# Second block's first norm without its plain total, weight splits one pair at a time, sines inside the feed-forward

## The reference, cut to what matters

```
# first block
h = x + mix(rms_norm(x, mix_norm_w)) @ w_out
h = h + (silu(gate) * up) @ w_down        # gate, up = rms_norm(h, ffn_norm_w) @ w_gate_up, width 2816
x1 = rms_norm(h, final_norm_w)            # = h * fin * r1,  r1 = (mean(h^2) + EPS)^-0.5
# second block
shift1, scale1, gate1, shift2, scale2, gate2 = split(silu(c) @ ada_w + ada_b)
hn = rms_norm(x1, norm1_gain) * (1 + scale1) + shift1
r_q, r_k, r_v, r_g, s_q, s_k, s_v = split(hn @ w_in)
y = [retention(rotary(r_q), rotary(r_k), r_v) ..., stick_breaking(rms(s_q), rms(s_k), s_v)]
x  = x1 + gate1 * (y @ w_out)
x  = x + gate2 * peer(rms_norm(x, norm2_gain) * (1 + scale2) + shift2)   # 8 heads, top 16 of 16384 experts
```

## Time and profile before

| | us |
|---|---|
| median of 3 runs | 1205.56 |
| lowest, highest | 1204.44, 1211.71 |
| the profiled execution, its own time | 1207.72 |
| its span, first to last instruction | 1205.1 |
| PE busy | 1034.2 (86%) |
| DVE busy | 886.5 (74%) |
| ACT busy | 435.6 (36%) |
| POOL busy | 288.7 (24%) |
| DMA, mean over the span | 314 GB/s |

### The profile page before, as it was taken

The page is one execution under the profiler, slowest core; times in us unless marked ns, Lnnn a source line. Parts: engine busy times, 40 slices in busy tenths (PEclk is TensorE's granted clock), DMA queues, the critical chain, the costliest instruction groups (busy, mean ns, idle before and its releaser), DMA issues.

```text
span 1205.1 us, 14407 instructions
## 1 busy us (share of the span) xinstructions
PE 1034.2 (86%) x5140; PEld 720.2 (60%) x5140; DVE 886.5 (74%) x1809; ACT 435.6 (36%) x845; POOL 288.7 (24%) x260
## 2 busy tenths in 40 slices
PE   6998989999999998977989976887687768777987
PEld 6888889999988876964546432333233323333343
DVE  6976679998759785688478777667776776677545
ACT  6645454434446646443233222222211222122112
POOL 0000000000000000033435643544355335434530
PEclk9998999999999999988989988988898889888998
DMA  9532449979818331069999999999999999999994
GB/s 364 183 140 88 140 182 351 352 284 339 312 45 319 124 108 68 1 230 384 420 385 403 422 421 421 422 421 421 421 422 421 421 421 421 422 421 422 422 421 179
DMA packets 67751, 378.59 MB, mean 314 GB/s; under 512 B 7521, under 2 KB 7777, under 8 KB 34913
## 3 DMA queue, kind: packets, MB, share of 16 engines
q0 software_dynamic: 36864, 268.45, 53.8%
q1 hardware_dynamic: 29952, 107.13, 24.6%
q10 hardware_dynamic: 864, 2.10, 0.5%
HBM read 376.61 MB, written 1.05 MB: 313 GB/s over the span
## 4 chain that ended last, share of the span: by engine, by line
PE 32%; DVE 30%; DMA 25%; ACT 7%; issue 5%; POOL 1%; SPq 0%; ACTq 0%; DVEq 0%
DMA ring_sb<-in_peer,idsb 16%; DVE ring_lo L1316 5%; PE pb L851 5%; PE pb L412 5%; PE pb L415 5%; PE pb L854 5%; DMA whi_rows<-in_peer,idsb 4%; DVE ring_sb L1845 3%; PE pb L440 3%; DMA arena<-in_peer,idsb 3%; DVE arena L1584 2%; ACT whi L890 2%; DMA xn<-in_peer,idsb 2%; DVE arena L1788 1%; DVE arena L1783 1%
## 5 line engine op out<-in xcount | busy, mean ns | idle before, releaser
L1908 POOL DMA_INDIRECT ring_sb<-in_peer,idsb x143 | 164.5, 1151 | 735.3 <-DVE idsb L1828 528.7
L412 PE MATMUL pb<-xhi,whi 128*128 128x256 f32 x928 | 240.9, 294 | 5.3 <-ACT xhi L916 1.5
L851 PE MATMUL pb<-ring_sb,arena 128*128 128x512 f32 x286 | 164.2, 658 | 84.8 <-ACT arena L1257 84.7
L415 PE MATMUL pb<-xlo,whi 128*128 128x256 f32 x928 | 234.9, 287 | 0.9 <-DVE xlo L1758 0.3
L1845 DVE CUSTOM_DVE_ANT_0 ring_sb<-ring_sb,arena 128x1024 f32<-128x1024 f32 x143 | 172.2, 1224 | 84.7 <-DMA ring_sb<-in_peer,idsb 84.6
L412 PEld LDWEIGHTS pb<-xhi,whi 128*128 128x128 f32 x928 | 179.5, 193 | 11.7 <-issue 8.2
L415 PEld LDWEIGHTS pb<-xlo,whi 128*128 128x128 f32 x928 | 179.8, 194 | 6.1 <-issue 3.3
L1316 DVE TENSOR_TENSOR ring_lo<-ring_sb,whi 128x1024 fp32r<-128x1024 f32 x138 | 161.5, 1220 | 21.5 <-ACT whi L890 21.5
L1252 ACT ACTIVATE arena<-arena 128x4 f32<-128x4 f32 (+1 forms) x70 | 14.4, 205 | 416.0 <-DVE arena L1845 416.0
L854 PE MATMUL pb<-ring_sb,arena 128*128 128x512 f32 x286 | 158.5, 638 | 0.0
L851 PEld LDWEIGHTS pb<-ring_sb,arena 128*128 128x128 f32 x286 | 58.3, 212 | 162.4 <-issue 162.4
(11 more groups left out here) (320 smaller groups left out, 1619.1 us busy)
## 6 DMA issues: line engine op xcount, KB each, us to landing
ring_sb<-in_ada SPq DMA_DIRECT2D x48, 512.0 KB, 5.3
ring_sb<-in_w_gu SPq DMA_DIRECT2D x44, 512.0 KB, 6.8
ring_sb<-in_w_in SPq DMA_DIRECT2D x40, 512.0 KB, 7.1
ring_sb<-in_w_down SPq DMA_DIRECT2D x22, 512.0 KB, 5.8
ring_sb<-in_w_out SPq DMA_DIRECT2D x16, 512.0 KB, 3.5
ring_sb<-in_w_q SPq DMA_DIRECT2D x16, 512.0 KB, 6.3
ring_sb<-in_peer,idsb POOLq DMA_INDIRECT x143, 22.5
ring_sb<-in_w_iv SPq DMA_DIRECT2D x4, 512.0 KB, 16.6
```

What stands on the lines that cost most here:

```text
L412: e.matmul(o, hi_w(u)[:, c], xh(k), start=start, stop=False, skip_group_check=skip)
L415: e.matmul(o, hi_w(u)[:, c], xl(k), start=False, stop=False, skip_group_check=skip)
L851: mm = e.matmul(pb[4 + 2 * tile][:, :], dgr[col % 16], o[:, 1024:1536], start=begin, stop=end)
L1908: e.indirect_dma_start(rows_at[s], None, peer, bass.IndirectOffsetOnAxis(ap=idsb[:, col:col + 1], axis=0)).then_inc(s_row[s], 16)
```

## The change

The plain total and everything on it leaves the norm: `wones` and `weighted_sums` are gone. ACT squares with the scale `finw` = sqrt(fin squared + EPS), made once in the first block, so that the squares are weighted already; DVE adds the slices, and `sums` makes the weighted total with two products. The plain total is made in the attention: ACT squares h into `x1s` (two 128x1024), DVE folds them to 256 columns (1024, 512, 256 wide), PE makes one product between `sb_pair(6)` and the next gemm, ACT its Ln and Exp. `scale_x1` moves behind the last stick-breaking step. In the group norms of queries and keys, each square follows its copy directly and only one pair of weights is split ahead (`take1`). The two DMAs of the sub-keys (L1098) move from the norm's end to behind the last of these pairs. The sines move into step 12 of the feed-forward, the cosine into step 14. The transpose of the second ada half and its reduction are now two places.

```diff
# pe
             def plain_sums():
-                b = where["n2"] = bank((AN, "n2l1"))
-                for k in range(KD):
-                    mm = e.matmul(pb[b][:, 0:T], c_("ones"), one_(sq, k), start=k == 0, stop=k == KD - 1)
-                mm.then_inc(*PN.up("n2"))
+                b = where["x1"] = bank((AN, "x1ln"))
+                e.wait_ge(*VN.at(("x1", "part", 2)))
+                e.matmul(pb[b][:, 0:T], c_("ones"), x1s[:, 0:T], start=True, stop=True).then_inc(*PN.up("x1"))
...
-                if i >= 2:
-                    weighted_sums(i - 2)
             ring[0] = [0, 1, 2, 3, 4, 5]
-            weighted_sums(2)
-            weighted_sums(3)
-            plain_sums()
+            sums("n2", (5, 8), (AN, ("n2", "ln")))
...
             sb_pair(6)
+            plain_sums()
             gemm(U_rk[2:4], ("rk", 1), (AR, ("rk", "raw", 1)), mid=lambda: rope_turn("rk", 0))
# act
             e.activation(la_, la_, ACT.Sqrt).then_inc(*AL.up("root"))
+            e.wait_ge(*VM.at("fin2"))
+            e.activation(finw, fin2, ACT.Sqrt).then_inc(*AM.up("finw"))
...
             e.preload_act_table_set(SIGM)
-            e.wait_ge(*VR.at("ang"))
-            e.activation(sinT[:, :], cosT[:, :], ACT.Sin).then_inc(*AR.up("sin"))
-            e.activation(one_(stdt, 1), cosT[:, :], ACT.Sin, scale=0.5).then_inc(*AR.up("sinh"))
-            e.preload_act_table_set(SIGM)
-            e.wait_ge(*VM.at("fin2"))
-            for k in range(KD):
-                e.activation(wones[:, kc(k)], c_("ones"), ACT.Copy, scale=fin2[:, k:k + 1]).then_inc(*AM.up(("wones", k)))
             for j in range(NF + 2):
...
+                if j == 12:
+                    e.wait_ge(*VR.at("ang"))
+                    e.activation(sinT[:, :], cosT[:, :], ACT.Sin).then_inc(*AR.up("sin"))
+                    e.activation(one_(stdt, 1), cosT[:, :], ACT.Sin, scale=0.5).then_inc(*AR.up("sinh"))
+                    e.preload_act_table_set(SIGM)
...
-            e.wait_ge(*PN.at(("n2", "w")))
-            e.activation(one_(stdt, 1), pb[where["n2", "w"]][:, 0:T], ACT.Ln, scale=1.0 / D, bias=c_("eps2")).then_inc(*AN.up("n2l2"))
...
-            e.wait_ge(*PN.at("n2"))
-            e.activation(one_(stdt, 0), pb[where["n2"]][:, 0:T], ACT.Ln, scale=1.0 / D, bias=c_("eps")).then_inc(*AN.up("n2l1"))
...
+            root("n2")
+            e.wait_ge(*AN.at(("n2", "ln")))
+            e.activation(r2, one_(stdt, 0), ACT.Exp, scale=-0.5).then_inc(*AN.up(("n2", "rstd")))
             e.wait_ge(*VM.at("mod0"))
             x_hi("n2", lambda k: mod[:, k:k + 1])
...
+            def take1(us):
+                la.take(us, False)
+                split(la.fill(la.now + 1))
+                la.used(2)
+
+            take1(U_sq[0:2])
             for i in range(2):
-                take(U_sq[2 * i:2 * i + 2])
-                if i:
-                    group_rms(("q", 0), ("first",), (half(sbq, 0), ("sq", 0)))
                 e.wait_ge(*USED.at(U_sq[2 * i + 1]))
                 e.activation(half(sbq, i), pb[where["sq", i]][:, :], ACT.Copy).then_inc(*AS.up(("sq", i)))
+                group_rms(("q", i), ("first",), (half(sbq, i), ("sq", i)), lambda: take1((U_sq[2:4], U_sk[0:2])[i]))
...
             take(U_sv[2:4])
+            e.wait_ge(*USED.at(U_dn[NF - 1]))
+            for i in range(2):
+                e.dma_start(sub[i], subk[:, i * 1024:(i + 1) * 1024]).then_inc(s_sub, 16)
...
             take(U_rq[0:2])
+            for i in range(2):
+                e.activation(x1s[:, i * 1024:(i + 1) * 1024], hT[:, i * 1024:(i + 1) * 1024], ACT.Square).then_inc(*AN.up(("x1", "sq", i)))
             copy_raw("rq", U_rq, 0)
...
             copy_raw("rk", U_rk, 1)
+            e.wait_ge(*PN.at("x1"))
+            e.activation(one_(stdt, 0), pb[where["x1"]][:, 0:T], ACT.Ln, scale=1.0 / D, bias=c_("eps")).then_inc(*AN.up("x1ln"))
+            e.wait_ge(*AN.at("x1ln"))
+            e.activation(r1, one_(stdt, 0), ACT.Exp, scale=-0.5).then_inc(*AN.up("r1"))
# dve
                 for n_ in (2 * i, 2 * i + 1):
                     e.tensor_tensor(hk(n_), hk(n_), one_(pb[4 + i], n_ % 2), ADD).then_inc(*VN.up(("dn", n_)))
+                    if n_:
+                        part("n2", n_ - 1)
...
-            take(U_sq[0:2])
+            take1(U_sq[0:2])
             ada_part(46)
             ada_part(47)
-            take(U_sq[2:4])
+            take1(U_sq[2:4])
             group_rms(("q", 0), vc("sbq"), half(sbq, 0))
-            scale_x1()
-            take(U_sk[0:2])
+            take1(U_sk[0:2])
             group_rms(("q", 1), vc("sbq"), half(sbq, 1))
+            turn_32(1)
+            take1(U_sk[2:4])
+            group_rms(("k", 0), vc("sbk"), half(sbk, 0))
             sums_of_32(1)
...
             rope_turn("rq", rq2, 0)
+            for i, n_ in enumerate((1024, 512, 256)):
+                e.wait_ge(*(VN.at(("x1", "part", i - 1)) if i else AN.at(("x1", "sq", 1))))
+                e.tensor_tensor(x1s[:, 0:n_], x1s[:, 0:n_], x1s[:, n_:2 * n_], ADD).then_inc(*VN.up(("x1", "part", i)))
             sb_pair(4)
...
             take(U_rv[2:4])
+            scale_x1()
```

More of the change, by code:

```diff
@@ L471, in sums @@
                 keep_clock(keep[1]) if keep[1] else None
-            def weighted_sums(i):
-                if i == 0:
-                    where["n2", "w"] = bank((AN, "n2l2"))
-                for k in (2 * i, 2 * i + 1):
-                    e.wait_ge(*AN.at(("n2", "sq", k)))
-                    mm = e.matmul(pb[where["n2", "w"]][:, 0:T], wones[:, kc(k)], one_(sq, k), start=k == 0, stop=k == KD - 1)
-                if i == 3:
-                    mm.then_inc(*PN.up(("n2", "w")))
             def plain_sums():
-                b = where["n2"] = bank((AN, "n2l1"))
-                for k in range(KD):
-                    mm = e.matmul(pb[b][:, 0:T], c_("ones"), one_(sq, k), start=k == 0, stop=k == KD - 1)
-                mm.then_inc(*PN.up("n2"))
+                b = where["x1"] = bank((AN, "x1ln"))
+                e.wait_ge(*VN.at(("x1", "part", 2)))
+                e.matmul(pb[b][:, 0:T], c_("ones"), x1s[:, 0:T], start=True, stop=True).then_inc(*PN.up("x1"))
             def residual(us8, name, steps_, between):
@@ L896, in square @@
             def square(name, k):
-                s = k if name == "n2" else sq_slot(k)
-                if k == 7 and name != "n2":
+                if k == 7:
                     e.wait_ge(*VN.at((name, "part", 1)))
-                e.activation(one_(sq, s), hk(k), ACT.Square).then_inc(*AN.up((name, "sq", k)))
+                e.activation(one_(sq, sq_slot(k)), hk(k), ACT.Square,
+                             scale=finw[:, k:k + 1] if name == "n2" else 1.0).then_inc(*AN.up((name, "sq", k)))
             def root(name):
                 e.wait_ge(*PN.at(name))
-                e.activation(stdt[:, 0:T], pb[where[name]][:, 0:T], ACT.Ln, scale=1.0 / D, bias=c_("eps")).then_inc(*AN.up((name, "ln")))
+                e.activation(stdt[:, 0:T], pb[where[name]][:, 0:T], ACT.Ln, scale=1.0 / D,
+                             bias=c_("eps2" if name == "n2" else "eps")).then_inc(*AN.up((name, "ln")))
             def inv_root(name):
@@ L1104, in group_rms @@
                 e.wait_ge(*AS.at(src[1]))
+                if name == ("q", 0):
+                    e.wait_ge(*PN.at("n2"))
                 e.activation(half(tmp, name[1]), src[0], ACT.Square).then_inc(*AS.up((name, "sq")))
+                if between:
+                    between()
                 e.wait_ge(*PS.at(name))
@@ L1612, in dve @@
                     if n_ == 23:
+                        turn_32(0)
                         sums_of_32(0)
@@ L1688, in dve, with take1 @@
             e.wait_ge(*VR.at("cos"))
-            take(U_sq[0:2])
+            def take1(us):
+                la.take(us, False)
+                split(la.fill(la.now + 1))
+                la.used(2)
+            take1(U_sq[0:2])
             ada_part(46)
             ada_part(47)
-            take(U_sq[2:4])
+            take1(U_sq[2:4])
             group_rms(("q", 0), vc("sbq"), half(sbq, 0))
-            scale_x1()
-            take(U_sk[0:2])
+            take1(U_sk[0:2])
             group_rms(("q", 1), vc("sbq"), half(sbq, 1))
+            turn_32(1)
+            take1(U_sk[2:4])
+            group_rms(("k", 0), vc("sbk"), half(sbk, 0))
             sums_of_32(1)
-            take(U_sk[2:4])
-            group_rms(("k", 0), vc("sbk"), half(sbk, 0))
-            take(U_sv[0:2])
+            take1(U_sv[0:2])
             group_rms(("k", 1), vc("sbk"), half(sbk, 1))
```

33 lines of the change are left out of this document (11 added, 22 removed).

## The result

The changed kernel takes 1193.66 us, the median of 4 runs (1192.57 to 1194.97), against 1205.63 us for the kernel before, the median of 4 (1204.44 to 1211.71). The ratio is 0.9893, 95% interval 0.9865 to 0.9921: about 12 us, 1.1%, faster. The forecast was 1195.2 in a range of 1190.5 to 1202. The profiled execution took 1192.57 us.

What follows compares the result with a forecast made beforehand. PE was taken to bound the feed-forward, PE and DVE the stick-breaking heads, DMA engines PEER at unchanged length. Terms summed to 10.4 us, taking the 1205.56 us median to 1195.2; range 1190.5 to 1202.

Steps and rivals of the forecast that it cites:

- start of the feed-forward: Feed-forward head: ACT splits weights sooner without sines and tiles, so PE regains its lost time; +5.4 us.
- weighted sums and norm: Norm between the blocks: four matmul records between down products go, +0.9 us; chain becomes the earlier norm's, +2.8 us.
- clock behind the norm: Behind the norm between the blocks: filling products and shorter waits keep PE's clock up; +1.2 us, bounds 0 and 1.7.
- group norms: Query and key norms: square directly behind copy takes ACT's splits out of PE's way; +3.0 us.
- plain total, additions and product: Stick-breaking heads: DVE's three additions are not hidden, -2.2 us; PE's product costs -0.5 us.
- sines in step 12, moved DMAs, `scale_x1`: Feed-forward step 12, sub-key loads, and scaling behind the last rests: work moved under cover; each costs 0.
- `finw`: First block: one small activation of 8 columns on ACT's path; -0.2 us.
- its cushion: Feed-forward: DVE's lead over PE, 0.8 us in step 3, some 0.1 behind transpose and reduction.
- Rival B: Feed-forward head gains nothing because the earlier start runs into late weights from DMA; 1200.6 us, chance 0.14.
- The rule that I had weighed against this term: Clock behind the norm: throttling is the default and release varies, so the dip could stay, making the term 0.
- Rival A: Stick-breaking heads: the plain total is free, 2.7 us of cost vanish; 1192.5 us, chance 0.18.
- Rivals C and D: C: one weight pair ahead comes too late, 1216.7 us, chance 0.05. D: sines block a feed-forward step, 1198.6, 0.05.

Runs made afterwards that it cites:

- experiment 3: The changed kernel with sines, their table load and the cosine back at the feed-forward's start, `wones` tiles still out; 1197.08 us, ratio 0.9931.
- experiment 2: The changed kernel with the group norms' old order, two pairs of weights split ahead, square behind the next pair's splits; 1197.96 us, ratio 0.9936.
- experiment 5: The changed kernel without DVE's three plain-total additions, only the first 256 of 2048 columns summed; 1191.02 us, ratio 0.9875.
- experiment 9: The late_total kernel with the plain total's product in bank 6 instead of the ring's next bank; 1189.94 us, ratio 0.9875.
- experiment 6: The changed kernel without the filling products around the sums of the norm between the blocks; 1196.43 us, ratio 0.9918.
- late_bank: Same run as experiment 9: late_total with the plain total's product in bank 6; 1189.94 us, ratio 0.9875.
- late_total: The changed kernel with plain-total additions behind the last stick-breaking head, its product ahead of the second block's output product, scaling behind the gating; 1195.04 us, ratio 0.9903.
- again_before: The kernel before the change, run once more with no edit; 1206.55 us, ratio 1.0007.
- head_sines: Same run as experiment 3: the changed kernel with the sines back at the feed-forward's start; 1197.08 us, ratio 0.9931.
- pool_adds: Same run as experiment 4: the changed kernel with the plain total's three additions on POOL; 1193.81 us, ratio 0.9897.
- no_filling: Same run as experiment 6: the changed kernel without filling products at the norm between the blocks; 1196.43 us, ratio 0.9918.
- fill_first: Same run as experiment 8: the changed kernel with nine filling products in the first block; 1192.13 us, ratio 0.988.
- late_bank_fill: Same run as experiment 10: late_bank with filling products at two more places; 1189.36 us, ratio 0.987.
- experiment 8: The changed kernel with nine filling products in the first block, behind the second pair of lru gate units; 1192.13 us, ratio 0.988.
- experiment 10: The late_bank kernel plus nine filling products in the first block and six ahead of the second block's output product; 1189.36 us, ratio 0.987.
- old_splits: Same run as experiment 2: the changed kernel with the group norms' old order; 1197.96 us, ratio 0.9936.
- no_adds: Same run as experiment 5: the changed kernel without DVE's three plain-total additions; 1191.02 us, ratio 0.9875.
- experiment 4: The changed kernel with the plain total's three additions on POOL instead of DVE; 1193.81 us, ratio 0.9897.

## Why the prediction was right, step by step

The forecast of 10.4 us stands against 10.45 in the five stretches it spoke of, and the medians are 12.0 apart. The mechanism of each term was right, but that the sum agrees to 0.1 us is luck: terms off by 0.4 to 0.8 us cancel.

| term | forecast | measured | by |
|---|---|---|---|
| start of the feed-forward | +5.4 | +5.26 | trace; sines alone 2.90 (3) |
| weighted sums and norm | +0.9 +2.8 | +0.85 +2.35 | trace |
| clock behind the norm | +1.2 | +1.18, of which +0.6 stays | 2 against before |
| group norms | +3.0 | +3.8 | 2 |
| plain total, additions and product | -2.2 -0.5 | -2.33 -0.42 | 5 against after; 5 against 9 |
| DVE's shorter wait in the same round | not forecast | +0.35 | 9 against before |
| sines in step 12, moved DMAs, `scale_x1` | 0 | 0 | trace |
| `finw` | -0.2 | -0.1 | ACT's timeline |

**Feed-forward.** Right, down to its cushion: the one step that is not 8.64 us (234.50 to 243.28, 8.78) shows that the margin, put at some 0.1 us behind the transpose and reduction, is used up by then. Rival B falls with it.

**The norm.** 0.45 us short, and the weighted sums 0.05: up to the last down product PE gained 0.85 us (336.82 to 346.70 before, 329.68 to 338.71 after), from there to the next product 2.35 (7.84 against 5.49). The prediction read its 7.52 and 4.74 us as from the last addition; both are from the last but one (a merged row, and 145.61 for the last one in the earlier norm), so their difference is of the same chain and stands. The chain after is 4.96 us, not 4.74, which is 0.22; the other 0.21 lie just ahead of it. In the kernel after, DVE makes additions to h and additions of slices in turn, one behind the other, and comes to the last but one 0.53 us behind the start of PE's last down product; before, it waited for PE there and came 0.32 us behind.

**Clock and group norms.** Together 4.2 forecast, 4.39 measured, but split wrongly. The clock's own loss was sized rightly, 1.18 us in the first three units. But the trace of before mixed the two: where ACT's squares hold PE, part of what a slow clock costs is hidden. Without the slow clock, in experiment 2, PE waited longer for the first square, 2.47 us in place of the 1.87 of the earlier trace rows. So the wait that I read off was too small a price for the order, by 0.6 us, and the clock's term too large by as much as long as the old order stands. The rule that I had weighed against this term, that the dip could also stay, did not come true in any of the nine profiles with the filling; in the three without it the dip came (both of before, and 6, where it cost 0.9 us).

**The plain total.** Both terms were right in size: the additions cost 2.33 us (forecast 2.2) and the product 0.42 (0.5). That the stretch lost only 2.40 comes from the 0.35 us by which DVE's wait got shorter, which was not forecast and whose cause is open. Rival A (the plain total free) is out as the change stands: PE waits 1.55 us for DVE. With the additions and the product moved it becomes true: 9 takes the whole 2.75 us away in the trace, and its median is 1189.94.

**Rivals C and D.** The one pair ahead was always in time: no wait on a split or rest at the start of a pair. The piece with the sines is 3.3 us on ACT, from 258.76 to the end of the load that starts at 260.80, and no step waits for it. The Trainium skill, "ScalarE: Activation LUTs", What ACT_TABLE_LOAD costs, gives a drain of 1.38 us beside each load; here the sine starts 0.02 us behind the end of its load and the loads of experiment 3 are 1.29 apart, so no such drain shows.

**What was not in the sum.** The remaining 1.5 us between 1195.2 and 1193.66 is too small to be told from the spread of the runs. In the profiled pair, the 5 us beyond the sum (15.4 of span) are unchanged code: 1.9 ahead of the feed-forward, where the clock's luck in the first block gave 2.8 and a later start took 1.0 back, and 3.0 in PEER. The prediction held PEER's length to be unchanged. It is 677.2 and 678.0 us in the two profiles of before and between 672.5 and 676.3 in the ten of the kernels with the change. No instruction differs there, but both profiles of before are the longest; two are too few to tell whether that is chance; if it is not, it could account for the 1.5 us.

## What to carry to other kernels

Where an engine gets its work back after a wait on ACT or DVE, look for the work that could be anywhere: here the sines, eight constant tiles and a plain total were wanted much later than they were made, and only where they stood was their price. A piece of work moved to a busy engine costs its full length there (2.3 us) and nothing at all in a place where the engine idles, but the move also changes who gets the next buffer of a ring: count the banks again before blaming the work. And where a slow clock and a late engine fall into the same stretch, their losses cannot simply be added from the trace; the wait is understated by what the slow clock has hidden in it (0.6 us here).

## What the runs showed that I had not expected

**The clock falls in some executions and not in others, at the same waits.** PE's wait of 2.54 to 2.55 us in the first block leaves the granted clock at 1.00 in one profile and at 0.87 and 0.50 in another (late_bank, 105 to 110 and 110 to 115 us); the stretch costs 6.56 to 9.59 us. Between 445 and 485 us seven of the eleven other profiles show such a fall and the kernel after none (late_total's, behind its longer wait, among them). At the wait ahead of the output product the way to the third norm's sums is 28.9 us with the fall (again_before, head_sines, pool_adds, no_filling, fill_first) and 27.4 without; between the first pair of retention gate units and the next unit the way is 12.6 us with the fall (head_sines, pool_adds, late_bank_fill) and 11.0 without. The Trainium skill, "TensorE: Matmul & The Clock Gate", Part 1, says that the moment at which the throttle is released varies from run to run; what varies in these rows is whether and when the clock falls. With filling products in PE's order ahead of such a wait, which took its time or most of it away, the clock stayed at 1.00 in the three places tried: at the norm between the blocks in nine of nine profiles, against none of three without; in the first block in two of two (8, 10), against one of ten; ahead of the output product in one (10), which is too few to tell, since five profiles without filling (before, after, old_splits, no_adds, late_bank) held it there too.

**POOL slows DVE.** The 1792 columns of additions took 5.69 us on POOL, 2.40 on DVE, and while they ran two instructions of DVE took 2.92 us instead of 0.89 (4).
